# Two unrolled layers, with the mixer fed by the unnormalised input and 1/rms applied at the evictions

## What is computed

```python
def rms_norm(x, g):
    return x * lax.rsqrt(jnp.mean(x * x, axis=-1, keepdims=True) + EPS) * g

def hybrid_mixer(h, w_in, ...):                     # h = rms_norm(x, norm_mix_g)
    pa, pq, pk, pv, pc, pg = jnp.split(h @ w_in, SPLITS, axis=-1)
    ya = conformer_branch(pa, ...)                  # GLU, 31-tap causal conv, layer norm, SiLU
    yb = diff_attention_branch(pq, pk, pv, ...)     # 4 heads, two softmaxes each
    yc = gmlp_branch(pc, ...)                       # GELU, layer norm, spatial product
    gates = jax.nn.sigmoid(pg + gate_b)
    return (gates[0] * (ya @ w_br[0]) + gates[1] * (yb @ w_br[1])
            + gates[2] * (yc @ w_br[2])) @ w_out

for l in range(2):
    x = x + hybrid_mixer(rms_norm(x, norm_mix_g[l]), ...)
    x = x + mem_cross_attention(rms_norm(x, norm_xattn_g[l]), mem, ...)
    x = x + conv_ffn(rms_norm(x, norm_ffn_g[l]), ...)
return rms_norm(x, norm_final_g)
```

## Time and profile before

| | us |
|---|---|
| median of 3 runs | 1882.19 (1882.07 to 1887.53) |
| the profiled execution | 1882.24 |
| its span, first to last instruction | 1880.1 |
| TensorE busy | 1804.2 (96%) |
| VectorE, ScalarE, POOL busy | 1182.7, 731.1, 480.1 |

### The profile page before, as it was taken

The page is one execution under the profiler, slowest core; times in us unless marked ns, Lnnn a source line. Parts: engine busy times, 40 slices in busy tenths (PEclk is TensorE's granted clock), DMA queues, the critical chain, the costliest instruction groups (busy, mean ns, idle before and its releaser), DMA issues.

```text
span 1880.1 us, 25698 instructions
## 1 busy us (share of the span) xinstructions
PE 1804.2 (96%) x8572; PEld 1497.7 (80%) x8572; DVE 1182.7 (63%) x1549; ACT 731.1 (39%) x936; POOL 480.1 (26%) x177
## 2 busy tenths in 40 slices
PE   5999999999989999999979999999999899999996
PEld 3898878888868788888868897888888687888885
DVE  5793655454438876586659746454643687776594
ACT  3224634433444532343332336443442533432342
POOL 0543000102104234444234410000030132434332
PEclk8999999999989999999989999999999999999998
DMA  7322122142301332322332222313222123322323
GB/s 260 145 96 107 68 85 106 68 144 103 123 35 69 111 112 90 112 90 90 113 136 90 90 91 74 118 68 135 90 102 100 46 90 112 113 90 90 113 90 135
DMA packets 28934, 192.67 MB, mean 102 GB/s; under 512 B 3544, under 2 KB 3672, under 8 KB 7548
## 3 DMA queue, kind: packets, MB, share of 16 engines
q1 hardware_dynamic: 26188, 175.46, 26.3%
q0 software_dynamic: 1792, 13.63, 2.0%
q10 hardware_dynamic: 816, 1.86, 0.3%
HBM read 183.52 MB, written 9.78 MB: 103 GB/s over the span
## 4 chain that ended last, share of the span: by engine, by line
PE 90%; DVE 3%; ACT 3%; issue 2%; POOL 1%; DMA 1%; ACTq 0%; DVEq 0%; POOLq 0%
PE ps L1241 26%; PE ps L1242 26%; PE ps L1251 25%; PE ps L1184 2%; PE ps L1186 2%; PE ps L1191 2%; PE ps L1277 2%; ACT x_hd L588 1%; PE ps L1295 1%; PE ps L1334 1%; PE ps L1150 1%; POOL rs L471 1%; DMA v_sb<-bs 1%; ACT merged L588 1%; DVE x_tl L803 1%
## 5 line engine op out<-in xcount | busy, mean ns | idle before, releaser
L1241 PE MATMUL ps<-x_hd,w_hd 128*128 128x512 f32 x1600 | 628.5, 393 | 13.6 <-DVE x_tl L775 7.9
L1242 PE MATMUL ps<-x_tl,w_hd 128*128 128x512 f32 x1600 | 625.2, 391 | 0.0
L464 POOL TENSOR_TENSOR w_tl<-raw,w_hd 128x2048 fp32r<-128x2048 f32 x78 | 359.4, 4608 | 519.3 <-ACT w_hd L588 391.5
L588 ACT ACTIVATE w_hd<-raw 128x2048 fp32r<-128x2048 f32 x158 | 303.1, 1918 | 353.3 <-PE ps L1242 295.2
L1251 PE MATMUL ps<-x_hd,w_tl 128*128 128x512 f32 x1600 | 381.3, 389 | 0.0
L1241 PEld LDWEIGHTS ps<-x_hd,w_hd 128*128 128x128 f32 x1600 | 301.9, 189 | 85.8 <-DVE x_tl L775 14.4
L1242 PEld LDWEIGHTS ps<-x_tl,w_hd 128*128 128x128 f32 x1600 | 302.0, 189 | 62.0
L1251 PEld LDWEIGHTS ps<-x_hd,w_tl 128*128 128x128 f32 x1600 | 300.2, 188 | 62.3
L770 DVE TENSOR_TENSOR w_tl<-raw,w_hd 128x2048 fp32r<-128x2048 f32 x80 | 183.4, 2293 | 239.1 <-ACT w_hd L588 137.0
L1241 PE MATMUL ps<-ring_hd,w_hd 128*128 128x512 f32 (+1 forms) x672 | 254.5, 383 | 3.1 <-DVE resid L1017 3.1
L1242 PE MATMUL ps<-ring_tl,w_hd 128*128 128x512 f32 (+1 forms) x672 | 252.2, 379 | 0.0
(11 more groups left out here) (151 smaller groups left out, 1550.9 us busy)
## 6 DMA issues: line engine op xcount, KB each, us to landing
raw<-units SPq DMA_DIRECT2D x160, 1024.0 KB, 4.8
resid_dram<-resid POOLq DMA_DIRECT2D x2, 2048.0 KB, 10.2
resid<-resid_dram POOLq DMA_DIRECT2D x2, 2048.0 KB, 9.4
resid<-x_t SPq DMA_DIRECT2D x4, 512.0 KB, 6.6
bias_t<-bias_tiles POOLq DMA_DIRECT2D x8, 256.0 KB, 3.5
cg<-mem_t POOLq DMA_DIRECT2D x2, 1024.0 KB, 5.5
out<-resid SPq DMA_DIRECT2D x4, 512.0 KB, 2.7
bias_rows<-strip_dram SPq DMA_DIRECT2D x1, 1280.0 KB
```

The costliest lines, as they stand in the source:

```text
L464: line.done(pool.tensor_tensor(w_tl[:, k % 2, :], raw[:, k % 2, :], w_hd[:, k % 2, :].bitcast(F32), ALU.subtract), f"tail{k}")
L588: line.done(act.activation(out, in_, func, **kw), *labels)
L1241: pe.matmul(dst, w_hd[:, slot, w], hd[:, src, :], start=kc == 0, stop=False)
L1242: i = pe.matmul(dst, w_hd[:, slot, w], tl[:, src, :], start=False, stop=False)
```

## The change

- The loops over the layers are unrolled, with constants in the waits; unit numbers g run over both layers (156), and units beyond the last are neither loaded nor split.
- The mixer's products take g*x in place of g*x/rms: `x_hd` and `x_tl` come straight from `resid`. 1/rms is spread to a tile `r0`, and VectorE multiplies by it when it evicts `ab`, `u`, `q`, `k` and the gates; ScalarE then does tanh and GELU from SBUF. `w` and `v`, which have tokens on the partitions, are evicted by ScalarE in four pieces each with `rs0` as the scale.
- Sums of squares of the mixer norm are column-summed in the middle of unit 0 and spread after it.
- In units 76 and 77 of the first layer heads, tails and squares of the next input are made as the last products of the feed-forward are evicted.
- Prologue: x's tiles and halves of unit 0 are loaded in turn; the spatial sums come after unit 0 in banks 4 and 5, the spatial biases on VectorE at the end of k = 1, and TensorE waits for them before unit 2, the first on those banks. Lambda, the bias tables and their DMAs are moved between the first units.
- The conv has twelve slots, and `CLN` is 13, so that centring, squares, sums and spread of the conv branch come one unit later; the attention jobs stay where they were.
- x needed again for layer 1 is read from the input; for layer 2 it is stored and read back as before.

```diff
-CLN = 12
+CLN = 13
...
-for _slot, _n in enumerate((13, 13, 13, 13, 13, 13, 13, 7, 8, 10, 8)):
+for _slot, _n in enumerate((12, 12, 12, 12, 12, 12, 12, 8, 8, 8, 8, 8)):
...
+            load_x(0)
+            sp.dma_start(raw[:, 0, 0:half], units[0][:, 0:half]).then_inc(half_in, 16)
+            load_x(1)
+            sp.dma_start(raw[:, 0, half:UNIT], units[0][:, half:UNIT]).then_inc(weights_in[0], 16)
+            load_x(2)
+            load_x(3)
+            sp.dma_start(raw[:, 1, :], units[1]).then_inc(weights_in[1], 16)
+            sp.dma_start(ident[:], ident_in).then_inc(ident_loaded, 16)
+            sp.dma_start(v_sb[:, 0:DEPTH, :], w_st).then_inc(ws_in, 16)
...
+                if g == 5:
+                    sp.wait_ge(vector_done, line.at((0, f"bs{DEPTH - 1}_3")))
+                    for lay in range(DEPTH):
+                        sp.dma_start(wsbs_dram[lay, 0], v_sb[:, lay, :]).then_inc(wsbs_out, 16)
+                        sp.dma_start(wsbs_dram[lay, 1], v_sb[:, DEPTH + lay, :]).then_inc(wsbs_out, 16)
...
+            for g in range(2, TOTAL):
+                sp.wait_ge(gpsimd_done if tail_by_pool(g - 2) else vector_done, line.at(of_unit("tail", g - 2)))
+                sp.dma_start(raw[:, g % 2, :], units[g]).then_inc(weights_in[g % 2], 16)
+                prepare(g)
...
+                power("n0", rs0, ms, 4)
...
+            def first_head(lay, t, *after):
+                op(x_hd[:, t, :], resid[:, t, :], ACT.Identity, ((lay, f"n0_head{t}"),), after,
+                   scale=col(lay, "g_mix", t))
+            def first_square(lay, tag, t, *after):
+                op(sq[:, t % 2, :], resid[:, t, :], ACT.Square, ((lay, f"{tag}_sq{t}"),),
+                   after + (((lay, f"{tag}_sum{t - 2}"),) if t >= 2 else ()))
+            act.wait_ge(pvec_in, 16)
+            half = UNIT // 2
+            for n in range(4):
+                act.wait_ge(x_in[n], 16)
+                for t in (2 * n, 2 * n + 1):
+                    first_head(0, t)
+                if n == 0:
+                    act.wait_ge(half_in, 16)
+                    op(w_hd[:, 0, 0:half], raw[:, 0, 0:half], labels=("half_head",))
+                if n == 1:
+                    act.wait_ge(weights_in[0], 16)
+                    op(w_hd[:, 0, half:UNIT], raw[:, 0, half:UNIT], labels=(of_unit("head", 0),))
             for t in range(KD):
-                act.wait_ge(x_in[t // 2], 16)
-                squares("x", lambda t: resid[:, t, :], (t,))
-            for n in range(2):
-                head_of_unit(n, f"head_u{n}", 16)
-            op(ld[:], ld[:], ACT.Exp, ("lam_exp",), ("lam_dot",))
+                first_square(0, "n0", t)
+                if t == 3:
+                    head_of_unit(1)
...
-                            op(tmp[:, arg % 2, :], ps[:, b + 1, :], ACT.Tanh, (f"th_ab{arg}",),
-                               (f"ev{ENTRY_OF['ab', arg - 2]}",) if arg >= 2 else (), scale=0.5)
+                            op(tmp[:, arg % 2, :], tmp[:, arg % 2, :], ACT.Tanh, (f"th_ab{arg}",), (f"ab_gate{arg}",),
+                               scale=0.5)
                         elif kind == "u":
-                            op(u_sb[:, 2 * arg:2 * arg + 2, :], both, ACT.Gelu_apprx_tanh, (f"ev{e}",))
+                            view = u_sb[:, 2 * arg:2 * arg + 2, :]
+                            op(view, view, ACT.Gelu_apprx_tanh, (f"gelu_u{arg}",), (f"ev{e}",))
                         elif kind in ("w", "v"):
                             dst, f = (vn, ACT.Gelu_apprx_tanh) if kind == "w" else (v_sb, ACT.Copy)
-                            for i in range(2):
-                                op(dst[:, 2 * i:2 * i + 2, 256 * arg:256 * arg + 256],
-                                   ps[:, b + i, :].rearrange("p (t c) -> p t c", t=2), f, (f"ev{e}",))
-                        elif kind in ("q", "k"):
-                            act.wait_ge(resid_out, l * 16 + 16)
-                            dst = q_sb if kind == "q" else k_sb
-                            op(dst[:, 2 * arg:2 * arg + 2, :], both, ACT.Copy, (f"ev{e}",),
-                               scale=0.125 if kind == "q" else 1.0)
+                            for t in range(TB):
+                                op(dst[:, t, 256 * arg:256 * arg + 256],
+                                   ps[:, b + t // 2, 256 * (t % 2):256 * (t % 2) + 256], f, (f"ev{e}",), ("n0_rs",),
+                                   scale=rs0[:, t:t + 1])
...
+                                view = tmp[:, gate_at(pos, j) + i, :]
+                                op(view, view, ACT.Tanh, (f"th_g{pos}_{j + i}",), (f"raw_g{pos}_{j + i}",),
+                                   scale=0.5, bias=col(l, "gate_b", BRANCH_OF[pos] * KD + j + i))
...
+                            if l + 1 < DEPTH:
+                                first_head(l + 1, t, f"r3_5_{t}")
+                                first_square(l + 1, "n0", t)
+                            else:
+                                first_square("end", "r3", t, f"r3_5_{t}")
...
+            def first_tail(lay, t):
+                op(lambda: dve.scalar_tensor_tensor(x_tl[:, t, :], resid[:, t, :], col(lay, "g_mix", t),
+                                                    x_hd[:, t, :].bitcast(F32), ALU.mult, ALU.subtract),
+                   (lay, f"n0_tail{t}"), needs=((lay, f"n0_head{t}"),), independent=1)
+            def first_sum(lay, tag, t):
+                if t:
+                    first = sq[:, 0, :] if t == 1 else ssum[:]
+                    op(lambda: dve.tensor_tensor(ssum[:], first, sq[:, t % 2, :], ALU.add), (lay, f"{tag}_sum{t}"),
+                       *(((lay, f"{tag}_sum0"),) if t == 1 else ()), *(((lay, f"{tag}_all"),) if t == KD - 1 else ()),
+                       needs=((lay, f"{tag}_sq{t - 1}"), (lay, f"{tag}_sq{t}")))
...
-            tail_of_unit(0, "tail_u0", "head_u0")
+            line.begin(0)
             dve.wait_ge(pvec_in, 16)
+            for t in range(KD):
+                dve.wait_ge(x_in[t // 2], 16)
+                first_tail(0, t)
+                if t == 3:
+                    for i, (a, w) in enumerate(((0, S), (S, NREL - S))):
+                        op(lambda: dve.tensor_copy(strip[:, a:a + w], ps[0:HEADS, 6 + i, 0:w]), "strip_copied",
+                           needs=("strip_ps", "strip_clear"))
+            for t in range(KD):
+                first_sum(0, "n0", t)
+                if t == 3:
+                    dve.wait_ge(weights_in[0], 16)
+                    dve.wait_ge(half_in, 16)
+                    tail_of_unit(0)
...
+            def spatial_biases():
+                dve.wait_ge(ws_in, 32)
+                for lay in range(DEPTH):
+                    for g in range(4):
+                        dst = v_sb[:, DEPTH + lay, P * g:P * g + P]
+                        c = _cols["gln_b"] + g
+                        op(lambda: dve.scalar_tensor_tensor(dst, ps[:, 4 + lay, P * g:P * g + P], pv_all[:, lay, c:c + 1],
+                                                            dst, ALU.mult, ALU.add), f"bs{lay}_{g}",
+                           needs=(f"wsum{lay}",), independent=1)
...
+                    tail_of_unit(1)
+                mean_square("n0", ms, 4, D)
+                op(lambda: dve.tensor_copy(r0[:], misc), "n0_r", needs=("n0b",))
...
+                            glu = cg[:, C_IN[arg], PAD:]
+                            op(lambda: dve.tensor_tensor(tmp[:, arg % 2, :], ps[:, b + 1, :], r0[:], ALU.mult),
+                               f"ab_gate{arg}", needs=(f"e{e}",))
+                            op(lambda: dve.tensor_tensor(glu, ps[:, b, :], r0[:], ALU.mult), f"ev{e}", independent=1)
+                            op(lambda: dve.scalar_tensor_tensor(glu, tmp[:, arg % 2, :], 1.0, glu, ALU.add, ALU.mult),
                                needs=(f"th_ab{arg}",))
+                        elif kind == "u":
+                            for i in range(2):
+                                op(lambda: dve.tensor_tensor(u_sb[:, 2 * arg + i, :], ps[:, b + i, :], r0[:], ALU.mult),
+                                   f"ev{e}", needs=(f"e{e}",), independent=i)
+                        elif kind == "q":
+                            if l:
+                                dve.wait_ge(resid_out, 16 * l)
+                            for i in range(2):
+                                op(lambda: dve.scalar_tensor_tensor(q_sb[:, 2 * arg + i, :], ps[:, b + i, :], 0.125, r0[:],
+                                                                    ALU.mult, ALU.mult), f"ev{e}", needs=(f"e{e}",),
+                                   independent=i)
+                        elif kind == "k":
+                            for i in range(2):
+                                op(lambda: dve.tensor_tensor(k_sb[:, 2 * arg + i, :], ps[:, b + i, :], r0[:], ALU.mult),
...
+                                op(lambda: dve.tensor_tensor(tmp[:, gate_at(pos, j) + i, :], ps[:, b + i, :], r0[:],
```

(36 more changed lines are left out.)

## The result

The changed kernel takes **1895.97 us** (median of 6 runs, 1894.62 to 1898.52); the kernel before, run beside it, 1883.79 (6 runs, 1882.07 to 1888.42). The ratio is 1.0061, 95% interval 1.0046 to 1.0076: slower by 0.6%. The prediction was 1891.5, range 1877 to 1902. The profiled execution took 1895.55 us; its span is 1893.8, 13.7 more than the span before.

A forecast was written before the change was run, and what follows sets the result against it. TensorE, busy 1804 of 1880.1 us, was taken as the bound, so only gaps and slow stretches could be won. 1882.2 - 11.1 - 13.0 - 0.9 + 17.3 + 15.8 + 1.2 = 1891.5 us; range 1877 to 1902.

The forecast's parts named there:

- start: Layer 1's opening: products need only g*x, not 1/rms, so unit 1 begins at 34.3 instead of 45.5; gain 11.1 us.
- change of layers: Between layers 1 and 2: 14.5 us from last product to second unit, where it took 27.5; gain 13.0 us.
- end: Kernel's end: VectorE's last sums cost +1.2 us, POOL's power without a tail beside it saves 2.1; gain 0.9 us.
- unit 2, gap and clock: Before unit 2, layer 1 only: TensorE waits 15.5 us for spatial biases queued on VectorE, plus 1.8 for the clock.
- unit 14, gap: Unit 14, each layer: TensorE waits 5.9 us for conv-branch sums, their squares queued behind head 0's exponentials on ScalarE.
- unit 14, clock: Behind the gap at unit 14: TensorE's lowered clock costs 2.0 us more in each layer.
- rest of the mixer and cross attention: Mixer: added VectorE evictions ahead of ScalarE's reads show only where chains are tight; loss 1.2 us, bounds 0 and 15.6.
- rival 3: VectorE bounds the mixer, TensorE waiting 1.3 us at each of twelve gated triples: 1907 us, with half 1899; chance 14%.
- list of signs: Forecast wrong if unit 2's wait is under 10 us, none follows unit 14, or gaps appear at units 15 to 31.
- Loop overhead is gone: Mixer: loop overhead disappears; its former cost was counted under the waits at the change of layers, with no separate term.
- Rival 1: Whole gains without new waits, biases and squares arriving in time: 1857 us; chance 6%.
- Rival 2: Shorter waits: GLU product not held, data 2 us sooner, unit 14 wait 4 us with clock up: 1879 us; 16%.

## Why the prediction was right in sum, and where its terms were off

Slower was right, and the two causes it named are the causes. The sum came out 4.5 us short of the median. That it came so near is partly luck: the clock at unit 14 and the rest of the mixer were some 12 us too low together, and the gap at unit 14 and the unseen power took back 7. By its own steps:

| term | predicted | profile after, and runs |
|---|---|---|
| start | -11.1 | -10.0 (unit 1 at 35.48 for 45.48) |
| change of layers | -13.0 | -13.4 |
| end | -0.9 | +0.3 |
| unit 2, gap and clock | +17.3 | +17.5; 17.1 when taken away |
| unit 14, gap | 2 x 5.9 | 2 x 4.3 |
| unit 14, clock | 2 x 2.0 | up to 2 x 5.1 |
| rest of the mixer and cross attention | +1.2 | +7 in waits |
| power ahead of the cross attention | not seen | -3.8 |

**Right in mechanism and size.** The wait at unit 2 is 15.4 us for 15.5, with each link of its chain as worked out; the GLU product, bounded by the twin of the earlier trace rows, ended 5.2 us after the unit for 5.3. The change of layers took 14.15 us for 14.5. The start was 1.2 us late at unit 1: the column sums began at 25.36 for 24.2, and the rest of the way came out right by two misses that cancel, as said above.

**Unit 14: the mechanism right, both sizes off.** The gap was too large because the chain was moved as a block behind the exponentials of the earlier trace rows. The exponentials ended 1.6 us earlier than that against TensorE, mostly since a table load of 1.28 us, which had stood between the scores and them, was now done at 207.23, while ScalarE waited for the scores. The clock term was too small because the earlier trace rows showed a gap followed by long products, and it was taken for every gap. Here small products follow, and the low time was 10.2 us and not 4.

**The end.** Its +1.2 came true, since the wait for the sums is 4.56 us for 3.39. The power is down to 1.0. But two things took back the gain: the column sums met a low clock (1.56 us for 1.05), and the last eight multiplications took 7.07 us for 6.23, with a gap of 0.46 among them. The spread ran at half clock in both kernels (2.08 and 2.04).

**The rest of the mixer** is the step that failed. It was put at 1.2 us with bounds of 0 and 15.6, on the ground that a gate's banks have 5.4 us to spare. The banks were indeed never waited for. But VectorE's lateness came out elsewhere: at the output product 1.57 and 1.21 us, at transposes 0.37 and 0.46. ScalarE, which now evicts v in four pieces, adds 0.48 twice at the spatial products. The cover named was that of the banks, and the chains through the attention and the merge have none. That is rival 3 of the prediction at a lower price and in other places; with the long waits mended and the repeated ones left in, it is 9 us. By the prediction's own list of signs, gaps at units 15 to 31 would show it wrong: there are two, the 0.37 and 0.46. Another part was not seen at all: the three cross waits grew by 1.2 us a layer, by instructions that wait for two semaphores. "Loop overhead is gone" left out what came in its place. The first list of semaphores above could be read before any run.

**The power** of before, 3.14 us, was in the list of the earlier trace rows as a maximum. The prediction asked only after the one at the end. It says that elsewhere TensorE runs without a gap up to unit 40, which is a misreading: the gap of 1.89 at 486.83 lies before that, and its twin in layer 2. Both hung on a start 0.04 or 0.05 us apart.

Rival 1 falls, since both waits are there. Rival 2 had the gap at unit 14 right (4 us) and the rest wrong: the product is held, and the clock does fall. The terms do not add up exactly: by the table the span grows by some 16 us, by the trace by 13.7. In the cross attention and behind it the kernel before had some 7 us more low time in each layer than the changed one (13.7 and 13.6 for 6.8 and 6.8), of which up to half counts; the two traces drift by some 4 us there. What then remains, 1 to 2 us of the other sign, is not assigned. The low time at the end of the span is much the same in both (14.4 and 14.8).

## What to carry to other kernels

If a factor can be applied at the evictions, the product can start before it is known: 22 us here for two places. List at once what shares a queue with the moved work, because one block of one-off instructions behind twelve others gave back 17. Put such one-off work and short norm chains ahead of longer work in their queue. When waits are taken out of a kernel whose clock falls and rises, compare the low time as well as the gaps before crediting or faulting the edit. And when a program is unrolled or its waits are planned, count the semaphores on each instruction of the engine that sets the pace, and drop those already waited for.

## What the runs showed of the hardware

- The same gap of 1.7 us left the clock at 1.00 in one kernel and took it to 0.60 over 4 us in another; the same small products with 0.3 us of gap or less left it up in layer 1 and took it down for 6.8 us in layer 2. What decides was not found.
- The clock alone is worth several us: low time was 76.3 us in the changed kernel and 91.5 in one with some 3 us less of waits, at the same total time. The same program ran in 1853 us at a mean clock of 0.991 and in 1861 at 0.986; the kernel before ranged from 1879 to 1890 with mean clocks from 0.986 to 0.977.
- A second semaphore on a ScalarE instruction costs 0.06 us of its pitch (0.66 for 0.60).
- POOL's power of 4 elements took 3.14 us when a VectorE tail began 0.04 us before it, and 1.03 when it began 0.19 us after it; the tail took 2.29 us both times.
- Ten products of 128x512 took 2.4 us, though a product's row is 0.39 long: at full clock they follow each other every 0.23, so a row's length is not the pitch.
